# A decoder layer on one core: the pools' linear map in three rounded passes, a projection's tail cut into 14 chunks, and the samples' products moved behind the attention work

## Time and profile before

| | |
|---|---|
| median of 3 runs | 2145.68 us (2144.77 to 2147.12) |
| profiled execution, its own time | 2146.32 us |
| its span, first to last instruction | 2144.5 us |
| TensorE products busy | 2099.0 us, 98% |
| VectorE, ScalarE, GpSimd busy | 890.0, 616.0, 243.7 us |
| mean granted clock of TensorE | 0.996 of full |

### The profile page before, as it was taken

The page is one execution under the profiler, slowest core; times in us unless marked ns, Lnnn a source line. Parts: engine busy times, 40 slices in busy tenths (PEclk is TensorE's granted clock), DMA queues, the critical chain, the costliest instruction groups (busy, mean ns, idle before and its releaser), DMA issues.

```text
span 2144.5 us, 36997 instructions
## 1 busy us (share of the span) xinstructions
PE 2099.0 (98%) x12759; PEld 2003.2 (93%) x12759; DVE 890.0 (42%) x2408; ACT 616.0 (29%) x2165; POOL 243.7 (11%) x389
## 2 busy tenths in 40 slices
PE   5999999999999999999999999999999999999999
PEld 3889999999999999999999999999999998998897
DVE  3543333334444344444431244132131247666664
ACT  4634333333333333333354111111121141111010
POOL 2222112111111121111100000000000000000000
PEclk9999999999999999999999999999999999999999
DMA  9756666664645646455244244255422356444441
GB/s 344 256 160 199 221 198 203 207 204 151 201 152 184 196 146 193 151 178 182 89 116 133 83 153 143 94 196 187 152 97 93 126 197 233 169 144 134 149 131 60
DMA packets 258633, 354.05 MB, mean 165 GB/s; under 512 B 24964, under 2 KB 230868, under 8 KB 257069
## 3 DMA queue, kind: packets, MB, share of 16 engines
q1 hardware_dynamic: 209849, 309.82, 43.9%
q10 hardware_dynamic: 48636, 42.33, 6.2%
HBM read 256.52 MB, written 183.77 MB: 205 GB/s over the span
## 4 chain that ended last, share of the span: by engine, by line
PE 92%; DVE 3%; SPq 2%; issue 1%; DMA 1%; ACT 1%; POOL 1%; ACTq 0%; DVEq 0%
PE a_pp L762 13%; PE a_pp L760 13%; PE a_pp L761 12%; PE pp L760 9%; PE pp L762 9%; PE pp L761 9%; PE c_pa L761 3%; PE c_pa L762 3%; PE c_pa L760 3%; PE c_py L761 3%; PE c_py L762 3%; PE c_py L760 2%; PE po L1598 2%; PE pqk L1564 1%; PE po L1597 1%
## 5 line engine op out<-in xcount | busy, mean ns | idle before, releaser
L760 PE MATMUL a_pp<-a_wH,hH 128*128 128x384 f32 x1520 | 528.5, 348 | 6.0 <-DVE qkv L1399 5.2
L762 PE MATMUL a_pp<-a_wH,hL 128*128 128x384 f32 x1520 | 516.2, 340 | 0.0
L761 PE MATMUL a_pp<-a_wL,hH 128*128 128x384 f32 x1520 | 514.2, 338 | 0.0
L760 PE MATMUL pp<-hH,next_H 128*128 128x412 f32 (+1 forms) x1040 | 369.9, 356 | 1.4 <-issue 1.4
L762 PE MATMUL pp<-hH,next_L 128*128 128x412 f32 (+1 forms) x1040 | 363.2, 349 | 0.0
L761 PE MATMUL pp<-hL,next_H 128*128 128x412 f32 (+1 forms) x1040 | 363.1, 349 | 0.0
L760 PEld LDWEIGHTS a_pp<-a_wH,hH 128*128 128x128 f32 x1520 | 287.1, 189 | 10.1 <-ACT qkv L1283 4.4
L761 PEld LDWEIGHTS a_pp<-a_wL,hH 128*128 128x128 f32 x1520 | 287.3, 189 | 0.0
L762 PEld LDWEIGHTS a_pp<-a_wH,hL 128*128 128x128 f32 x1520 | 286.2, 188 | 0.0
L1277 ACT ACTIVATE a_junk<-a_pp 128x128 f32<-128x128 f32 x384 | 106.6, 278 | 545.1 <-PE a_pp L762 539.0
L1388 DVE TENSOR_SCALAR a_ms<-a_ss 128x2 f32<-128x2 f32 (+1 forms) x204 | 34.5, 169 | 524.5 <-ACT a_junk L1277 524.4
(11 more groups left out here) (259 smaller groups left out, 3158.2 us busy)
## 6 DMA issues: line engine op xcount, KB each, us to landing
out_dram<-in_state_kv_w_dram SPq DMA_DIRECT2D x64, 1023.5 KB, 5.9
qkv_dram<-qkv SPq DMA_DIRECT2D x192, 192.0 KB, 2.1
qkv_in<-qkv_dram SPq DMA_DIRECT2D x192, 192.0 KB, 2.6
a_wst<-in_w_in_dram SPq DMA_DIRECT2D x38, 512.0 KB, 7.3
gl<-gT_dram SPq DMA_DIRECT2D x64, 264.0 KB, 3.9
out_dram<-in_state_kv_w_dram SPq DMA_DIRECT2D x8, 2044.0 KB, 11.3
gT_dram<-ost ACTq DMA_DIRECT2D x72, 206.0 KB, 2.6
next_st<-in_w_in_dram SPq DMA_DIRECT2D x26, 512.0 KB, 5.6
```

Source lines behind the costliest of these rows:

```text
L760: nc.tensor.matmul(out, sH, mH, start=(i == 0), stop=False)
L761: nc.tensor.matmul(out, sH, mL, start=False, stop=False)
L762: last = nc.tensor.matmul(out, sL, mH, start=False, stop=(i == len(terms) - 1))
```

## The change

It has three parts.

1. **Pools.** VectorE rounds `mixed` to a high part (in the place of the `run` buffer that the group's last sum doesn't use) and subtracts for the low part; once, it does the same for the weights. The linear map is a `three_pass`.
2. **z_a's tail.** The two column groups are cut into 7 chunks each of 296 tokens; only step 218 has no chunk.
3. **Samples.** A sample's product goes to the free 384 columns of the values' bank that was not written last, and stands at the end of its step, behind the values, on TensorE, ScalarE and VectorE alike. Blocks alternate between the two `pp` banks among themselves. On VectorE, `lows` moves from the end of a step to the place behind `mean`.

```diff
+            wpool_L = scope(same_place)[0]("wpool_L", [P, 4, P], F32R)
         wpool = sb("wpool", [P, 4, P])
...
+            wpool_H = scope(same_place)[0]("wpool_H", [P, 4, P], F32R)
...
+                    run_H.append(scope(same_place)[0](f"run_H{i}", [P, TT], F32R, side="right"))
...
+        def mixed_H(p):
+            return run_H[(p + 1) % 2][:, :]
...
-                    nc.vector.scalar_tensor_tensor(mixed[:, SEQ:TT], s_sum[:, 1, :], 1.0 / w, u_s, ALU.mult,
-                                                   ALU.subtract).then_inc(mix_ready, 1)
+                    chained(nc.vector.scalar_tensor_tensor(mixed[:, SEQ:TT], s_sum[:, 1, :], 1.0 / w, u_s, ALU.mult, ALU.subtract))
+                    chained(nc.vector.tensor_copy(mixed_H(p), mixed[:, :]))
+                    nc.vector.tensor_tensor(mixed_L[:, :], mixed[:, :], mixed_H(p).bitcast(F32), ALU.subtract).then_inc(mix_ready, 1)
...
+                dve.wait_ge(pool_in, 32)
+                chained(nc.vector.tensor_copy(wpool_H[:, :, :], wpool[:, :, :]))
+                nc.vector.tensor_tensor(wpool_L[:, :, :], wpool[:, :, :], wpool_H[:, :, :].bitcast(F32), ALU.subtract).then_inc(pool_ready, 1)
...
-                        nc.tensor.matmul(ppool[m % 2][:, 0:width(c)], wpool[:, p, :], mixed[:, cols_of(c)],
-                                         start=True, stop=True).then_inc(pool_done, 1)
+                        three_pass(nc, ppool[m % 2][:, 0:width(c)], [(wpool_H[:, p, :], wpool_L[:, p, :], mixed_H(p)[:, cols_of(c)],
+                                                                      mixed_L[:, cols_of(c)])]).then_inc(pool_done, 1)
...
+    block_steps = [s for s in range(STEPS) if plan[s][1] != SAMP]
+
+    def used_last(s):
+        same = sample_steps if plan[s][1] == SAMP else block_steps
+        n = same.index(s) - (1 if plan[s][1] == SAMP else 2)
+        return same[n] if n >= 0 else None
...
-    TAILS = len(TAIL) * NBC
+    TAIL_CHUNKS = (ALL + DRAIN - 2 - STEPS) // len(TAIL)
+    TCH = 4 * -(-TT // (4 * TAIL_CHUNKS))
+    TAILS = len(TAIL) * TAIL_CHUNKS
...
-    bare = [left[(i + 1) * len(left) // (len(left) - TAILS + 1)] for i in range(len(left) - TAILS)]
+    bare = [left[(i + 1) * len(left) // (len(left) - TAILS) - 1] for i in range(len(left) - TAILS)]
...
+        def bank(s):
+            return po[beside_values(s)][:, P:] if plan[s][1] == SAMP else pp[block_steps.index(s) % 2]
+
+        def values_by(s):
+            return [j for j in range(NB) if slots[j] + 3 <= s]
+
+        def beside_values(s):
+            return 1 - values_by(s)[-1] % 2 if values_by(s) else 0
...
             for s in range(ALL + DRAIN):
-                if s < STEPS:
+                if s in block_steps:
                     mean(s)
+                if s in at_slot:
+                    lows(at_slot[s])
...
-                if s in at_slot:
-                    lows(at_slot[s])
+                if s in sample_steps:
+                    mean(s)
+                    normalise(s)
...
             def project(s):
                 u, b = plan[s]
-                if s >= 2:
-                    pe.wait_ge(act_read, s - 1)
-                    pe.wait_ge(qk_normed, s - 1)
+                if used_last(s) is not None:
+                    pe.wait_ge(act_read, used_last(s) + 1)
+                    pe.wait_ge(qk_normed, used_last(s) + 1)
                 if b == SAMP:
                     if s == sample_steps[0]:
                         pe.wait_ge(samp_step, 2)
+                        pe.wait_ge(h_mod, NH)
+                    if values_by(s):
+                        pe.wait_ge(o_evac, values_by(s)[-1])
...
+                for n, s in enumerate(sample_steps):
+                    if beside_values(s) == j % 2 and s < slots[j] + 3 and (j < 2 or slots[j - 2] + 3 <= s):
+                        pe.wait_ge(samp_summed, (n + 1) * (CG - 1))
...
                 if s - 3 in at_slot:
                     values(at_slot[s - 3])
+                if s in sample_steps:
+                    project(s)
```

More of the change, by code:

```diff
@@ L158, in finish @@
         ost = [sb(f"ost{i}", [P, BCH]) for i in range(NBC)]
+        with ExitStack() as same_place:
+            wpool_L = scope(same_place)[0]("wpool_L", [P, 4, P], F32R)
         wpool = sb("wpool", [P, 4, P])
@@ L183, in finish @@
             uT = pool_sb("uT", [P, PADU + TT], side="right")
-            run = [pool_sb(f"run{i}", [P, PADU + SEQ], side="right") for i in range(2)]
+            run, run_H = [], []
+            for i in range(2):
+                with ExitStack() as same_place:
+                    run_H.append(scope(same_place)[0](f"run_H{i}", [P, TT], F32R, side="right"))
+                run.append(pool_sb(f"run{i}", [P, PADU + SEQ], side="right"))
+            with ExitStack() as same_place:
+                mixed_L = scope(same_place)[0]("mixed_L", [P, TT], F32R, side="right")
             mixed = pool_sb("mixed", [P, TT], side="right")
             zS = pool_sb("zS", [P, TT], side="right")
+        def mixed_H(p):
+            return run_H[(p + 1) % 2][:, :]
         ol, cw = combine_tiles(both_sb)
@@ L217, in finish @@
         out_stored = [sem(f"out_stored{i}") for i in range(NBC)]
-        pool_in, turned, spT_ready, pad_ready = (sem_again(n) for n in ("pool_in", "turned", "spT_ready", "pad_ready"))
+        pool_in, turned, pool_ready, pad_ready = (sem_again(n) for n in ("pool_in", "turned", "pool_ready", "pad_ready"))
         window, mix_ready, pool_done, biased, gated, tail_saved, tail_ready = (
@@ L921, in tail_cols @@
     def tail_cols(n):
-        c = n % NBC
-        return slice(c * BCH, min((c + 1) * BCH, TT))
+        c = n % TAIL_CHUNKS
+        return slice(c * TCH, min((c + 1) * TCH, TT))
     stack = ExitStack()
@@ L1260, in project_read @@
                 rows = P if b < BLOCKS else NS
-                src = pp[s % 2] if b < BLOCKS else s_part
+                src = bank(s) if b < BLOCKS else s_part
                 act.wait_ge(proj_done, s + 1)
@@ L1383, in mean @@
                             dve.wait_ge(samp_summed, n * (CG - 1) + j - 1)
-                        nc.vector.tensor_tensor(s_part[:, :], pp[s % 2][j * QUAD:j * QUAD + NS, 0:3 * P], s_part[:, :], ALU.add).then_inc(samp_summed, 1)
+                        nc.vector.tensor_tensor(s_part[:, :], bank(s)[j * QUAD:j * QUAD + NS, 0:3 * P], s_part[:, :], ALU.add).then_inc(samp_summed, 1)
                 dve.wait_ge(squared, 2 * s + 2)
@@ L1527, in project @@
                         for j in range(CG):
-                            last = nc.tensor.matmul(pp[s % 2][j * QUAD:j * QUAD + NS, 0:3 * P], hs_t[:, k + j, :], side(k + j),
+                            last = nc.tensor.matmul(bank(s)[j * QUAD:j * QUAD + NS, 0:3 * P], hs_t[:, k + j, :], side(k + j),
                                                     start=(i == 0), stop=(i == len(rounds) - 1))
@@ L1548, in tail_product @@
                 if n < 2:
-                    pe.wait_ge(act_read, STEPS + n - 1)
-                    pe.wait_ge(qk_normed, STEPS + n - 1)
+                    pe.wait_ge(act_read, block_steps[n - 2] + 1)
+                    pe.wait_ge(qk_normed, block_steps[n - 2] + 1)
                 else:
```

18 lines of the change are left out of this document (9 added, 9 removed).

## The result

The changed kernel takes 2155.92 us (median of 5 runs, 2154.81 to 2160.76), the kernel before 2145.68 beside it: a ratio of 1.0052, with a 95% interval of 1.0038 to 1.0065. That is **10.2 us slower**. The forecast was 2151.7: the sign was right and the time lies in the range, but 4 of the 10 us were not foreseen. The profiled execution took 2155.57 (span 2153.8), 9.25 more than that of before.

What follows compares the result with a forecast made beforehand. TensorE, busy 98% of the span, was taken as the bound; pools -2.6, tail +2.1, later samples +7.7, early samples -1.2 sum to +6.0, giving 2151.7 us by the median, range 2143.5 to 2156.5 (forecast's own 2148.5 to 2156.5).

Steps and rivals of the forecast that it cites:

- Part 1: Pools' linear map: three passes of 0.56 us replace 0.69 on 20 chunks, VectorE's extra passes hidden; 2.6 us less.
- Part 2: z_a's tail: ScalarE, with two table loads a step, bounds steps at 5.1 us, not TensorE's 4.4; 2.1 us more.
- eleven steps of 5.1: z_a's tail: the full steps in the sum over ScalarE's list, 56.1 us together.
- Part 3, later: Nine later sample steps: moved products bare TensorE's waits, 9.7 us lost less 2.0 of waits removed; 7.7 us more.
- (c): Sample steps: no added cost, because subtracting first ends each chain earlier; 7.7 falls away, 2144.0 us; chance 0.10.
- (d): Tail and sample steps: both (a) and (c) hold, 2137.7 us; chance 0.05.
- Part 4, early: Early samples: two waits and a low clock go, partly lost to a late block load; 1.2 us less.
- So 2.4 of the 5.1 are left: Early samples: gain remaining once TensorE meets the third block load, expected at 157.9 but wanted at 155.
- (a): z_a's tail: ScalarE is not the bound, the tail gives -4.2; 2145.4 us, no slower; chance 0.15.
- (b): Early samples: block loads land in time, the full 5 us is gained; 2147.9 us; chance 0.10.
- (e): Ten sample steps: idle stretches drop the clock each time, 1.6 x 10 us more; 2167.7 us; chance 0.07.
- (f): z_a's tail: a function switch holds ScalarE twice as long as the load seen, 33 us more; 2185 us; chance 0.01.

Runs made afterwards that it cites:

- with Tanh: The kernel before with the 14-chunk tail, Silu made from Tanh and two VectorE passes, rows stored from one piece at the next step's start: 2141.20 us, ratio 0.9979.
- quick stores: The kernel before with the 14-chunk Silu tail, its rows stored from one piece of 1184 bytes: 2147.11 us, ratio 1.0006.
- part 2 alone: The kernel before with only the change to z_a's tail (14 chunks with Silu): 2149.15 us, ratio 1.0016.
- the repairs: The changed kernel with sample products in front, ScalarE's copy first up to the last projection, Tanh and one-piece rows, third unit's weights three blocks later: 2131.85 us.
- one variant: The kernel before with the samples part only, the sample's product at the start of its step on TensorE, still in the values' bank: 2154.59 us, ratio 1.0038.

## Why the prediction came out as it did

- **Part 1** held: 2.57 to 2.68 measured in the four profiled executions whose clock did not fall there, 2.6 forecast, with VectorE's passes hidden.
- **Part 2**: the mechanism was right, ScalarE with two table loads a step, and the runs show it from both sides (5.10 with Silu, 4.50 for TensorE with Tanh). The step that failed is the sum from ScalarE's list alone, "eleven steps of 5.1" and "the last has only a copy and a Silu, 1.6". Measured: eleven steps of 5.17, 0.8 more together, and a last one of 1.97 for 1.6; the step ahead of them took 4.80 for 4.6, for a cause that stays open (4.83 with quick stores too, 4.50 with part 2 alone). So the tail cost 3.57 in place of 2.1. The sum left out the stores: what a Silu waits for besides its chunk is its place, which the store of two chunks earlier has to free. That store takes 6.1 us; two full steps of 5.2 hide it, the short last ones don't. With quick stores the steps are 5.10, the last one 1.15, and the tail costs 1.57.
- **Part 3, later**: right in mechanism and nearly in size. The six steps with a look back cost 1.03 to 1.12 each (forecast 1.0); the three earlier ones 1.34, 0.88 and 1.53, together 3.75 (3.7). About 2.0 came back two steps on (2.0). Rivals (c) and (d) fell.
- **Part 4, early**: the gain of the two waits and the clock was right (5.2 at step 21). The step that failed is "So 2.4 of the 5.1 are left": nothing was left. Step 22 took 5.4 more than before, from the last product of step 21 to that of step 23; the forecast had about 3.9. The load landed 4.0 after its issue and not 3.3, a second load was late by 0.57, and the fall of the clock, of which half was counted, came whole (an estimate of 1.7 from the two stretches above: 0.30 of 3.1 and 0.21 of 3.7). The 3.3 is the median of ten loads, and for one load in a known place that was the wrong row. The same load of the kernel before, issued at 155.84 behind the same weights, has this line by itself:

```profile
DMA to landing us min/median/max: 4.0/4.0/4.0
```

- **The profiled execution**: that of before stood 0.64 above its median, that of after 0.35 below. Of the 10.2 between the medians, the stretches explain 9.25; the remaining 1 is the spread between executions, for which no term of the sum stood but the 0.64.
- Rivals (a) and (b) are what the repairs later made true: with Tanh, TensorE bounds the tail; with the weights out of the queue, the loads are issued early enough. In the change as it is, neither was. Rival (e) fell: from 242 to 1098, over all nine later sample steps with their waits, the longest 0.94, the granted clock was 1.00. With waits of 2.0 to 2.4 in these steps, as one variant had them, it came true three times of five. Rival (f) fell: a switch held ScalarE for the load's 1.28 and no more, since two of them fit in a step of 5.10.

## What to carry to other kernels

A product that looks like an interruption may be the cover of the waits around it; before moving it, ask which chain of other engines runs out under it, and move the *reading* behind instead, into a bank that nobody else wants soon. For each instruction in a sum list everything that it waits for, the place of its output too, with the landing time of the store that frees it: a slow store hides under long steps and shows at the short one. Where the trace has the very transfer or step that a sum needs, take its own row and not the median of its kind. And when a variant comes out as bad as what it mends, look at its steps before dropping the theory: a new wait may have taken the place of the old.

## What was not expected of the hardware

- The landing time of a store went with its pieces and not with its bytes alone: 6.1 us for 148 KB in pieces of 296 bytes and for 206 KB in pieces of 412, 1.9 us for 148 KB in pieces of 1184.
- A queue's work can hold the issue of a later, smaller transfer: 3.37 us on SP for a store that mostly takes 0.32 to 0.52.
- Almost equal waits had different consequences: 2.47 us was followed by a granted clock of 0.57 over 4 us, 2.35 us in the same place by 1.00; within one execution, 2.03 us was followed by 0.50 over 3.4 us and 2.03 us by 1.00. So waits of this length had a price of nothing or of about 1.6 beside their own.
